# The expert down products of a mixture-of-experts stage in three rounded passes instead of one full fp32 pass

## What is computed

```python
expert = (grp[:, None] * EXPERTS_PER_GROUP + top_e).reshape(-1)
...
def expert_block(args):
    xb, e = args
    return (jax.nn.silu(xb @ w1[e]) * (xb @ w3[e])) @ w2[e]
ys = lax.map(expert_block, (buf.reshape(n_blocks, MOE_BLOCK, d), block_e)).reshape(padded_rows, d)[dest]
```

## Time and profile before

| | us |
|---|---|
| median of the three executions | 3724.31 (3723.46 to 3726.82) |
| the profiled execution, its own time | 3726.51 |
| span of its profile | 3724.6 |
| TensorE busy in the span | 3312.6 |
| VectorE busy | 1811.9 |
| ScalarE busy | 1243.9 |

### The profile page before, as it was taken

The page is one execution under the profiler, slowest core; times in us unless marked ns, Lnnn a source line. Parts: engine busy times, 40 slices in busy tenths (PEclk is TensorE's granted clock), DMA queues, the critical chain, the costliest instruction groups (busy, mean ns, idle before and its releaser), DMA issues.

```text
span 3724.6 us, 34562 instructions
## 1 busy us (share of the span) xinstructions
PE 3312.6 (89%) x13568; PEld 2320.0 (62%) x13568; DVE 1811.9 (49%) x2689; ACT 1243.9 (33%) x1864; POOL 44.4 (1%) x76
## 2 busy tenths in 40 slices
PE   7987678789999976899899899999799978969997
PEld 3644676467667653658664378877577755438786
DVE  5335554256566544513562145554598855133343
ACT  2215113255555533215242122222422254032233
POOL 0000000000000000000000000000000000000000
PEclk9998889889999997999899999999899966989999
DMA  8420001379999962212013125541122210103220
GB/s 287 153 96 1 1 1 65 140 293 385 384 379 390 376 252 101 91 68 91 23 46 113 62 76 190 189 151 62 43 79 88 91 68 1 68 23 113 79 79 23
DMA packets 146798, 486.12 MB, mean 131 GB/s; under 512 B 8176, under 2 KB 11888, under 8 KB 134128
## 3 DMA queue, kind: packets, MB, share of 16 engines
q1 hardware_dynamic: 130544, 438.58, 31.6%
q10 hardware_dynamic: 10368, 24.79, 1.7%
q0 software_dynamic: 5760, 20.97, 1.4%
HBM read 459.15 MB, written 25.17 MB: 130 GB/s over the span
## 4 chain that ended last, share of the span: by engine, by line
PE 83%; DVE 8%; ACT 4%; issue 3%; DMA 1%; SPq 0%; POOL 0%; POOLq 0%; ACTq 0%; DVEq 0%; PEldq 0%
PE bank L456 15%; PE bank L458 14%; PE bank L457 14%; PE bank L355 14%; PE bank L1603 5%; PE bank L1114 3%; PE bank L2182 2%; PE bank L553 2%; PE bank L2766 2%; PE bank L545 1%; PE bank L2788 1%; PE bank L1571 1%; DMA ring<-in_w_ada 1%; PE bank L2776 1%; PE bank L2626 0%
## 5 line engine op out<-in xcount | busy, mean ns | idle before, releaser
L457 PE MATMUL bank<-h_parts,A_parts 128*128 128x512 f32 x1424 | 561.3, 394 | 0.0
L355 PE MATMUL bank<-A,ring 128*128 128x512 f32 x800 | 350.0, 600 | 15.1 <-DVE A L1260 8.4
L456 PE MATMUL bank<-h_parts,A_parts 128*128 128x512 f32 x816 | 323.4, 396 | 35.9 <-DVE h_parts L2984 13.4
L458 PE MATMUL bank<-h_parts,ring_parts 128*128 128x512 f32 x848 | 333.8, 394 | 0.0
L445 ACT ACTIVATE A_parts<-ring 128x1024 fp32r<-128x1024 f32 x162 | 170.4, 1053 | 420.9 <-PE bank L458 420.1
L457 PEld LDWEIGHTS bank<-h_parts,A_parts 128*128 128x128 f32 x1424 | 271.7, 191 | 58.6 <-issue 3.8
L452 DVE TENSOR_TENSOR ring_parts<-ring,A_parts 128x1024 fp32r<-128x1024 f32 x162 | 198.0, 1223 | 205.4 <-ACT A_parts L445 205.4
L355 PEld LDWEIGHTS bank<-A,ring 128*128 128x128 f32 x800 | 153.9, 193 | 209.4 <-issue 193.0
L1642 DVE TENSOR_TENSOR ring_parts<-ring,h_parts 128x1024 fp32r<-128x1024 f32 x192 | 225.7, 1221 | 42.7 <-ACT h_parts L1705 41.9
L458 PE MATMUL bank<-h_parts,A_parts 128*128 128x512 f32 x576 | 227.6, 395 | 0.0
L456 PE MATMUL bank<-A_parts 128*128 128x512 f32 x544 | 214.8, 395 | 5.3 <-DVE A_parts L2492 5.2
(11 more groups left out here) (493 smaller groups left out, 5398.5 us busy)
## 6 DMA issues: line engine op xcount, KB each, us to landing
ring<-in_expert_w SPq DMA_DIRECT2D x64, 2048.0 KB, 9.3
ring<-in_w_in SPq DMA_DIRECT2D x37, 2048.0 KB, 7.9
A<-in_expert_w SPq DMA_DIRECT2D x32, 2048.0 KB, 9.4
ring<-in_w_ada SPq DMA_DIRECT2D x24, 2048.0 KB, 12.4
ring<-in_w_ff SPq DMA_DIRECT2D x16, 2048.0 KB, 7.6
slot_rows<-A ACTq DMA_DIRECT2D x32, 512.0 KB, 9.2
ring<-in_w_ffn_gate SPq DMA_DIRECT2D x5, 2048.0 KB, 7.7
ring<-in_w_ffn_up SPq DMA_DIRECT2D x5, 2048.0 KB, 7.9
```

Source lines behind the costliest of these rows:

```text
L355: mm = pe.matmul(bank[tile % 4][:], ring_tile(g)[:, k, m * P:(m + 1) * P], rhs(k), start=(k == 0), stop=(k == g.kt - 1))
L456: pe.matmul(out, parts(w_high), parts(r_low), start=start, stop=False)
L457: pe.matmul(out, parts(w_high), parts(r_high), start=False, stop=False)
L458: return pe.matmul(out, parts(w_low), parts(r_high), start=False, stop=stop)
```

## The change

The down product takes the way of the inward products. w2 of each block is cut into four pieces that go through the same four places `moe_high(a)`, behind the pieces of the last inward matrix. The transposed gated rows are no longer copied by VectorE (L1661) but split behind their transposes: ScalarE copies the high part out of the bank (new `hid_copy`), then VectorE writes bank minus high to a new tile `hid_low` (`hid_split`). Per pair of blocks TensorE runs 48 rounded passes in place of 16 fp32 matmuls; ScalarE gets 8 highs and 2 copies more; VectorE gets 8 lows more and 2 splits in place of 2 copies. Semaphore counts follow. SyncE's order of loads is unchanged. The core of the diff:

```diff
-        MOE_IN = ((0, 0), (0, 1), (1, 0), (1, 1))
+        MOE_IN = ((0, 0), (0, 1), (1, 0), (1, 1), (0, 2), (1, 2))
...
+        hid_low = lambda s: W(43 + s)
...
-            def down(i, s, c):
-
-                if c == 0:
-                    pe.wait_ge(sem("moe_hid_t"), 2 * i + (s + 1))
-                    pe.wait_ge(sem(f"moe_w2{s}"), 16 * i)
-                    pe.wait_ge(sem("moe_y_read"), 2 * i + (s + 1))
-                wt = moe_w(s, 2).rearrange("p (f n) -> p f n", f=4)
-                for f in range(4):
-                    mm = pe.matmul(bank[2 * s + c][:], hid_t(s)[:, f * P:(f + 1) * P],
-                                   wt[:, f, c * 512:(c + 1) * 512], start=(f == 0), stop=(f == 3))
-                if c == 1:
-                    mm.then_inc(sem("moe_downed"), 1)
+            def down(i, s, pieces=range(4)):
+
+                for f in pieces:
+                    if f == 0:
+                        pe.wait_ge(sem("moe_hid_t"), 2 * i + (s + 1))
+                        pe.wait_ge(sem("moe_y_read"), 2 * i + (s + 1))
+                    pe.wait_ge(sem("moe_low"), 24 * i + (4 * s + f + 1))
+                    for c in range(2):
+                        n = slice(c * T, (c + 1) * T)
+                        mm = three_passes(pe, bank[2 * s + c][:], head(hid_t(s), f), head(hid_low(s), f),
+                                          moe_high(f)[:, n], moe_raw(4 + s, f)[:, n], f == 0, f == 3)
+                    mm.then_inc(sem("moe_downed" if f == 3 else "moe_used"), 1)
...
             with pe.Fori(1, n) as i:
-                down(i, 0, 0)
+                down(i, 0, (0, 1))
                 hid_turn(i, 1, 2)
-                down(i, 0, 1)
+                down(i, 0, (2, 3))
                 rows_turn(i, 0)
-                down(i, 1, 0)
-                down(i, 1, 1)
+                down(i, 1)
                 inward(i)
...
-            def hid_copy(i, s, back=0):
-                dve.wait_ge(sem("moe_hid_turned"), 2 * i + (s + 3 - back))
-                dve.tensor_copy(hid_t(s), bank[4 + 2 * s][:]).then_inc(sem("moe_hid_t"), 1)
-
-            def inward(i):
+            def hid_split(i, s, back=0):
+                dve.wait_ge(sem("moe_hid_high"), 2 * i + (s + 3 - back))
+                dve.tensor_tensor(parts(hid_low(s)), bank[4 + 2 * s][:], parts(hid_t(s)), ALU.subtract)\
+                    .then_inc(sem("moe_hid_t"), 1)
+
+            def down(i):
+
+                gate(i, 1, 2)
+                low(i, -2)
+                hid_split(i, 1, 2)
+                low(i, -1, (0, 1, 2))
+
+            def inward(i, after=False):
                 rows_split(i, 0)
+                if after:
+                    low(i, -1, (3,))
                 low(i, 0)
...
                 low(i, 2, (3,))
                 low(i, 3, (0,))
-                hid_copy(i, 0)
+                hid_split(i, 0)
                 low(i, 3, (1, 2, 3))
...
             with dve.Fori(1, n) as i:
-                gate(i, 1, 2)
-                hid_copy(i, 1, 2)
-                inward(i)
+                down(i)
+                inward(i, True)
...
+            def hid_copy(i, s, back=0):
+                act.wait_ge(sem("moe_hid_turned"), 2 * i + (s + 3 - back))
+                act.activation(parts(hid_t(s)), bank[4 + 2 * s][:], ACT.Copy).then_inc(sem("moe_hid_high"), 1)
...
                 silu(i, 0)
                 high(i, 2)
+                hid_copy(i, 0)
                 high(i, 3)
                 silu(i, 1)
...
             with act.Fori(1, n) as i:
+                high(i, -2)
+                hid_copy(i, 1, 2)
+                high(i, -1, (0, 1, 2))
                 y_copy(i, 0)
                 rows_copy(i, 0)
+                high(i, -1, (3,))
                 y_out(i, 0)
                 high(i, 0)
                 y_copy(i, 1)
                 y_out(i, 1)
                 inward(i)
+            high(n, -2)
+            hid_copy(n, 1, 2)
+            high(n, -1)
```

More of the change, by code:

```diff
@@ L1503, in build @@
         rows_low = lambda s: A[:, 37 + 2 * s:39 + 2 * s, :].rearrange("p a n -> p (a n)")
-        MOE_IN = ((0, 0), (0, 1), (1, 0), (1, 1))
+        MOE_IN = ((0, 0), (0, 1), (1, 0), (1, 1), (0, 2), (1, 2))
         moe_high = lambda a: h[:, 2 * a:2 * a + 2, :].rearrange("p a n -> p (a n)")
         moe_raw = lambda m, a: moe_w(*MOE_IN[m])[:, 2 * a * T:2 * (a + 1) * T]
-        moe_done = lambda m: sem(f"moe_{('gated', 'upped')[MOE_IN[m][1]]}")
+        moe_done = lambda m: sem(f"moe_{('gated', 'upped', 'downed')[MOE_IN[m][1]]}")
         hid = lambda s: W(24 + s)
@@ L1562, in moe_pe @@
             pe.wait_ge(*seen("slot_tokens", 1))
-            for name in ("gated", "upped", "downed", "rows_free", "used", "hid_turned"):
+            for name in ("gated", "upped", "downed", "rows_free", "hid_turned"):
                 pe.sem_inc(sem(f"moe_{name}"), 2)
+            pe.sem_inc(sem("moe_used"), 8)
             def rows_turn(i, s):
@@ L1580, in gated @@
                 for a in pieces:
-                    pe.wait_ge(sem("moe_low"), 16 * i + (4 * m + a + 1))
+                    pe.wait_ge(sem("moe_low"), 24 * i + (4 * m + a + 9))
                     for k in (2 * a, 2 * a + 1):
@@ L1620, in moe_pe @@
             with pe.Fori(1, n) as i:
-                down(i, 0, 0)
+                down(i, 0, (0, 1))
                 hid_turn(i, 1, 2)
-                down(i, 0, 1)
+                down(i, 0, (2, 3))
                 rows_turn(i, 0)
-                down(i, 1, 0)
-                down(i, 1, 1)
+                down(i, 1)
                 inward(i)
-            down(n, 0, 0)
+            down(n, 0, (0, 1))
             hid_turn(n, 1, 2)
-            down(n, 0, 1)
-            down(n, 1, 0)
-            down(n, 1, 1)
+            down(n, 0, (2, 3))
+            down(n, 1)
         def moe_dve(dve):
@@ L1637, in moe_dve @@
                 dve.sem_inc(sem(f"moe_{name}"), 2)
+            dve.sem_inc(sem("moe_low"), 8)
             def low(i, m, pieces=range(4)):
                 for a in pieces:
-                    dve.wait_ge(sem("moe_high"), 16 * i + (4 * m + a + 1))
-                    dve.tensor_tensor(parts(moe_raw(m, a)), moe_raw(m, a), parts(moe_high(a)), ALU.subtract)\
+                    dve.wait_ge(sem("moe_high"), 24 * i + (4 * m + a + 9))
+                    raw = moe_raw(m % 6, a)
+                    dve.tensor_tensor(parts(raw), raw, parts(moe_high(a)), ALU.subtract)\
                         .then_inc(sem("moe_low"), 1)
@@ L1677, in moe_dve @@
             with dve.Fori(1, n) as i:
-                gate(i, 1, 2)
-                hid_copy(i, 1, 2)
-                inward(i)
-            gate(n, 1, 2)
-            hid_copy(n, 1, 2)
+                down(i)
+                inward(i, True)
+            down(n)
+            low(n, -1, (3,))
         def moe_act(act):
@@ L1686, in moe_act @@
             act.sem_inc(sem("moe_y_read"), 4)
-            act.sem_inc(sem("moe_silu"), 2)
+            for name, v in (("silu", 2), ("high", 8), ("hid_high", 2)):
+                act.sem_inc(sem(f"moe_{name}"), v)
             for s in range(2):
@@ L1693, in high @@
             def high(i, m, pieces=range(4), fresh=False):
-                s, j = MOE_IN[m]
+                s, j = MOE_IN[m % 6]
                 for a in pieces:
                     if a == 0:
-                        act.wait_ge(sem(f"moe_w{j}{s}"), 16 * i + 16)
+                        act.wait_ge(sem(f"moe_w{j}{s}"), 16 * i + (16 if m >= 0 else 0))
                     if not fresh:
                         if a < 3:
-                            act.wait_ge(sem("moe_used"), 12 * i + (3 * (m - 1) + a + 3))
-                        elif m:
-                            act.wait_ge(moe_done(m - 1), 2 * i + (MOE_IN[m - 1][0] + 3))
-                        else:
-                            act.wait_ge(moe_done(3), 2 * i + 2)
-                    act.activation(parts(moe_high(a)), moe_raw(m, a), ACT.Copy).then_inc(sem("moe_high"), 1)
+                            act.wait_ge(sem("moe_used"), 18 * i + (3 * (m - 1) + a + 7 + 2))
+                        else:
+                            before = (m - 1) % 6
+                            act.wait_ge(moe_done(before), 2 * i + (MOE_IN[before][0] + (3 if m >= 1 else 1)))
+                    act.activation(parts(moe_high(a)), moe_raw(m % 6, a), ACT.Copy).then_inc(sem("moe_high"), 1)
+            def hid_copy(i, s, back=0):
+                act.wait_ge(sem("moe_hid_turned"), 2 * i + (s + 3 - back))
+                act.activation(parts(hid_t(s)), bank[4 + 2 * s][:], ACT.Copy).then_inc(sem("moe_hid_high"), 1)
             def rows_copy(i, s):
```

## The result

The changed kernel takes 3761.9 us (3756.9 to 3766.0 in four executions) against 3724.0: the ratio is 1.010, 95% interval 1.0082 to 1.0117. It is slower by 38 us. Four more executions, with their own runs of the kernel before, gave 3757.7 us and 1.0075 (1.0058 to 1.0092). The profiled execution took 3766.0, with a span of 3763.8.

What follows compares the result with a forecast made beforehand. TensorE was taken to set the pace, with the DMA engines just behind. Waits net of shorter work (+16.5 us) plus the clock (+5.5) made +22 us, forecast as 3746 us, range 3728 to 3764.

Steps and rivals of the forecast that it cites:

- the stands: TensorE's waits in and around the loop, net of its shorter work: +1.05 us per pass, +16.5 us together.
- the clock: Lower granted clock behind the wait at the gate: half the passes, 8 x 0.7 = +5.5 us.
- The prices and TensorE's own work: Trace durations per instruction and hop; TensorE's work falls 2.85 us per loop pass, leaving 35.4 us.
- Step 1: Block 1's gate precedes w2's first low on VectorE, so TensorE waits before the down product: 2.32 us.
- Step 3: Second w2's fourth piece comes late, behind ScalarE's copies and VectorE's split of the rows: TensorE waits 0.78 us.
- Step 5: Block 0's hid_copy sits before block 1's w3 highs on ScalarE, delaying two lows: TensorE waits 0.48 and 0.38 us.
- The rival that I gave 0.2: Clock falls behind every wait at the gate, costing its full 1.5 us: +22 us, 3763 us; chance 0.2.
- The faster rival: A w2 low ready at block 1's gate lets TensorE through; DMA at 398 GB/s limits it to 3702; chance 0.07.

Runs made afterwards that it cites:

- the last stand's experiment: Changed kernel with two w2 lows ahead of the gate and the turned rows' copy moved later, plus second w2's fourth piece ahead of rows' copy and split: 3687.8 us.
- the three mended kernels: Changed kernel with two w2 lows ahead of the gate, 3703.1 us; also turned rows' copy later, 3691.1; also second w2's fourth piece earlier, 3687.8.
- nine and four idle passes: Changed kernel with nine or four unused rounded passes put into TensorE's stand ahead of the down product: 3741.6 and 3739.7 us.

## Why the prediction was right, and where it was off

The forecast was slower, 3746 in 3728 to 3764; measured 3762, near the upper end. The mechanism held: the down product loses its cover at the gate, and the clock falls behind that stand. That the number lies in the range is owed to its upper end, which was set by a rival, more than to the sum: the stands were forecast at 16.5 us and took 13.2 (11.7 in the loop, 1.5 around it), the clock at 5.5 and took 18.7, and 7.3 us lie outside the stage, where nothing was forecast.

*The prices and TensorE's own work* held. A pass without a stand would be 35.4 us by the sum, and the kernel of the last stand's experiment, which has almost none, takes 35.7.

*Step 1, the gate*: shown. TensorE loses 2.26 us, forecast 2.32. That is counted from 1031.92, where the next pass would have started in a full pipeline (0.23 behind the last, at 1031.69), to 1034.18, where a full-speed first pass would have had to start for the third to start at 1034.63; the row's 1.99 leaves out the overlap of the matmuls and the slow first pass. With two lows in front it goes.

*Step 3*: 0.44 us, not 0.78. In the timeline of the same pass, from ScalarE's copy of the turned rows (1039.16) to TensorE's fourth piece (1047.05, with its slow start 1047.16) it was 8.00 us where I had 8.26: three highs up to y_copy took 2.84 us in place of 3.02, and from the low's end to TensorE it was 0.15 in place of 0.25. The other 0.09 is TensorE, which was ready that much later.

```profile
1039.66 2.94 ACT L1717 ACTIVATE h_parts<-A 128x1024 fp32r<-128x1024 f32 x3
...
1042.50 1.07 ACT L1739 ACTIVATE A<-bank 128x512 f32<-128x512 f32 x2
...
1047.05 0.50 PE L456 MATMUL bank<-A_parts 128*128 128x512 f32 x1 [0.17 <-DVE A_parts L1644]
```

*Step 5*: 0.42 and 0.35 us, forecast 0.48 and 0.38. In the changed kernel's timeline, beside the earlier trace rows (the 0.42; the 0.35 follows at 1027.70):

```profile
1023.11 0.60 ACT L1721 ACTIVATE A_parts<-bank 128x512 fp32r<-128x512 f32 x1 [2.13 <-PE bank L1594]
...
1023.60 3.89 ACT L1717 ACTIVATE h_parts<-A 128x1024 fp32r<-128x1024 f32 x4
...
1024.69 1.23 DVE L1644 TENSOR_TENSOR A_parts<-A,h_parts 128x1024 fp32r<-128x1024 f32 x1 [1.52 <-ACT h_parts L1717]
...
1025.44 0.39 PE L458 MATMUL bank<-h_parts,A_parts 128*128 128x512 f32 x1
...
1025.97 0.50 PE L456 MATMUL bank<-A_parts 128*128 128x512 f32 x1
```

ScalarE stands for 2.13 us before the copy, VectorE for 1.52 behind it, and TensorE's next pass starts 0.53 us after the last where 0.23 is the rule, and is slow itself. Moving the copy brought 36.80 - 35.97 = 0.83 us per pass, where the two stands are 0.77.

A pass at full clock was 39.1 us, not 39.37, so the loop lost 11.7 us by the stands where I had 15.8.

*The clock* is the term that was mis-sized: 5.5 us forecast, 18.7 measured. Both factors were wrong. I took 8 passes of 15, it was 12. And I let the stand of step 3 take up 0.78 of the 1.5 us, "since pieces come late there anyway". That step of the argument failed. The slow passes lie between the stand and hid_turn (1035.3 to 1038.3 in the rows above), and the pieces of step 3 come late because ScalarE's copy and highs start at hid_turn: they slide with it, the stand is 0.44 us in slow passes too, and nothing is absorbed. The rival that I gave 0.2, with +22 us for the clock and 3763 in all, was the nearest to the result. That it came within 1 us is luck: its 22 and 16.5 us are 6.6 too many together, and stand in for the 7.3 us outside the stage that it has no term for.

The Trainium skill (TensorE: Matmul & The Clock Gate, HAM oscillation) describes a loss that is paid anew in each tile of a loop; 12 of 15 passes here are closer to that than my half.

*The faster rival* was right in its mechanism and its place, the order ahead of the gate, and too modest in its bound: the share of 0.97 to 1.00 in the windows was no limit at 398 GB/s. The share is the time that packets took, and at a share of 0.99 to 1.00 the rate still rose without a late load (398, 407 and 409 GB/s in the three mended kernels, from 900 to 1200 us), and to 417 with late ones.

*The rest* (3.9 us ahead of the stage, mostly the clock as shown above, and 3.4 behind it in the profile, which the second profile of the same kernel does not have) was in no term of mine.

## What to carry to other kernels

A product that is slow on TensorE can be what hides the other engines' latencies; before it is made faster, write out for each in-order engine what stands in front of the first piece that TensorE will need. Put work that waits for TensorE's newest result (a gate, a copy out of a bank) behind one or two pieces that are ready, on every engine that feeds TensorE. And count a repeated stand of 2 us as more than 2 us: here the clock added 1.6 in four passes of five, and nothing in any pass with a stand of 1.5.

## What the runs showed of the hardware

- Stands of 1.08 and 1.53 us in a busy loop left the granted clock at 1.00 in each pass; with 1.98 us, 12 of 15 were followed by some 3 to 4 us at 0.50, in two executions in the same passes, and the three without a fall were six passes apart.
- The last stand, of 1.98 to 1.99 us behind the loop, was followed by the lower clock in four of five profiles (both of the changed kernel, nine and four idle passes; not two).
- Matmuls whose result nothing uses kept the clock at 1.00 through the loop, which was worth 18.7 us here. Two per stand were enough.
- With a DMA share of 0.99 to 1.01 the rate was 398, 407, 409 and 417 GB/s in kernels that asked for more and more (mean of 900 to 1200 us); up to 409 no load was late.
